# Seven products for a fourth pair of K tiles in every up strip, and two weight remainders made by an adding transfer

## The reference

```python
h += 0.5 * post(SwiGLU_1(pre(h)))      # swiglu(x) = (silu(g) * u) @ w_down, [g, u] = x @ w_up
h +=       post(Mixer(pre(h)))
h += 0.5 * post(SwiGLU_2(pre(h)))
```

## Time and profile before

| | us |
|---|---|
| median of 3 runs | 2366.02 (2365.82 to 2367.51) |
| the profiled execution | 2365.93 |
| its span, first to last instruction | 2364.2 |
| PE, DVE, ACT, POOL busy | 2349.9, 1823.2, 1265.4, 207.0 |
| share of the 16 DMA engines: SP's queue, GpSimd's queue | 59.5%, 3.5% |

### The profile page before, as it was taken

How to read it: one execution, slowest core, us unless ns; L and a number is a source line. 1 busy time by engine, 2 the same in 40 slices (tenths; PEclk the granted TensorE clock), 3 DMA queues, 4 the chain that set the end, 5 groups by cost and what they waited for, 6 DMA issues and landing times. The chain is left out here.

```text
span 2364.2 us, 34093 instructions
## 1 busy us (share of the span) xinstructions
PE 2349.9 (99%) x10579; PEld 1938.5 (82%) x10579; DVE 1823.2 (77%) x2163; ACT 1265.4 (54%) x1519; POOL 207.0 (9%) x402
## 2 busy tenths in 40 slices
PE   9999999999999999999999999999999999999998
PEld 7888888888888888888888888888888888888887
DVE  5999999978876655656675767665799999997886
ACT  6555555555545554454555544544655555555553
POOL 1212112110000000000000000000021212111000
PEclk9999999999999999999999999999999999999999
DMA  7666676665676565565565566666666666666665
GB/s 236 218 212 206 216 222 215 220 214 192 207 242 210 159 182 172 160 188 158 178 200 192 195 195 203 194 240 198 204 210 225 213 214 207 218 213 214 205 204 196
DMA packets 267183, 481.64 MB, mean 204 GB/s; under 512 B 21217, under 2 KB 54673, under 8 KB 265457
## 3 DMA queue, kind: packets, MB, share of 16 engines
q1 hardware_dynamic: 252752, 453.04, 59.5%
q0 software_dynamic: 14192, 27.73, 3.5%
q10 hardware_dynamic: 176, 0.07, 0.0%
HBM read 462.93 MB, written 6.29 MB: 198 GB/s over the span
## 5 line engine op out<-in xcount | busy, mean ns | idle before, releaser
L1382 ACT ACTIVATE w_hi<-w_raw 128x1024 fp32r<-128x1024 f32 (+1 forms) x848 | 857.4, 1015 | 926.1 <-PE acc L843 627.9
L1778 DVE TENSOR_TENSOR w_lo<-w_raw,w_hi 128x1024 fp32r<-128x1024 f32 (+1 forms) x848 | 984.2, 1164 | 420.0 <-ACT w_hi L1382 415.5
L841 PE MATMUL acc<-w_hi,xT_hi 128*128 128x512 f32 x1376 | 540.9, 393 | 1.2 <-DVE w_lo L1778 1.0
L843 PE MATMUL acc<-w_hi,xT_lo 128*128 128x512 f32 x1376 | 535.9, 389 | 0.0
L842 PE MATMUL acc<-w_lo,xT_hi 128*128 128x512 f32 x1376 | 535.7, 389 | 0.0
L841 PEld LDWEIGHTS acc<-w_hi,xT_hi 128*128 128x128 f32 x1376 | 258.3, 188 | 56.7 <-issue 3.0
L843 PEld LDWEIGHTS acc<-w_hi,xT_lo 128*128 128x128 f32 x1376 | 258.3, 188 | 54.4
L842 PEld LDWEIGHTS acc<-w_lo,xT_hi 128*128 128x128 f32 x1376 | 258.4, 188 | 52.2
L753 POOL DMA_DIRECT2D act_raw<-blocks x352 | 174.9, 497 | 736.3 <-DVE blocks L2114 646.9
L841 PE MATMUL acc<-w_hi,act_hi 128*128 128x512 f32 x560 | 218.2, 390 | 0.1
L842 PE MATMUL acc<-w_lo,act_hi 128*128 128x512 f32 x560 | 217.9, 389 | 0.0
(11 more groups left out here) (321 smaller groups left out, 2866.0 us busy)
## 6 DMA issues: line engine op xcount, KB each, us to landing
w_raw<-in_ffn_up_dram SPq DMA_DIRECT2D x352, 512.0 KB, 4.2
w_raw<-in_ffn_down_dram SPq DMA_DIRECT2D x176, 512.0 KB, 4.2
w_raw<-in_w_gate_dram SPq DMA_DIRECT2D x96, 512.0 KB, 4.4
w_raw<-in_w_in_dram SPq DMA_DIRECT2D x72, 512.0 KB, 3.7
w_raw<-in_w_in_dram SPq DMA_DIRECT2D x128, 256.0 KB, 3.0
w_raw<-in_w_ret_out_dram SPq DMA_DIRECT2D x32, 512.0 KB, 4.1
w_raw<-in_w_out_dram SPq DMA_DIRECT2D x32, 512.0 KB, 4.5
act_raw<-blocks POOLq DMA_DIRECT2D x352, 32.0 KB, 3.8
```

The source lines that it names most:

```text
L841: pe.matmul(pair[m][:, :], xh, wh, start=(first and kk == 0), stop=False)
L843: mm = pe.matmul(pair[m][:, :], xl, wh, start=False, stop=(last and kk == KG - 1))
L1382: act.activation(w_hi[:, s, cols], w_raw[:, s, cols], ACT.Copy).then_inc(w_rounded, 1)
L1778: dve.tensor_tensor(w_lo[:, s, cols], w_raw[:, s, cols], w_hi[:, s, cols].bitcast(f32), ALU.subtract).then_inc(w_split, 1)
```

## The change

Four K pairs of every up strip are quads: groups 5+6, 7+8, 10+11, 12+13 (slots 1+2, 3+0, 2+3, 0+1). The plain groups are gate 0 to 3 and upper 4, 9, 14, 15.

Groups 9 and 14 ("added" groups) take another way. GpSimd loads their raw weights into buffers of their own (`far_raw`) once PE has used the same group of the strip before. ACT rounds from there into `w_hi`, and earlier (at n = 1 and n = 7) writes the negated rounded part into `far_lo` in one more activation. Then a transfer on GpSimd's queue adds `far_raw` to `far_lo`, which gives raw - hi, the remainder; PE waits for it at the group. DVE skips these two groups, SP only counts them as landed. GpSimd's order in a strip is: two loads, the 16 transfers of the hidden strip, two adding transfers.

Left out of the diff below: buffer addresses and semaphores; the token sums of four pairs instead of three (two transposes more in the section `first` of each SwiGLU); the slices of `w_raw` that `sum13` and `sum24` read, now that one quad lies in slots 3 and 0; the wait of `hidden_hi` in the last strip, on quad 2 instead of 1.

```diff
@@ -51,9 +51,12 @@
-QUADS = ((5, 6, 5), (9, 10, 6), (12, 13, 7))
-PLAIN_GATE = ((0, 0), (1, 1), (2, 2), (3, 3), (4, 4))
-PLAIN_UP = ((7, 0), (8, 1), (11, 2), (14, 3), (15, 4))
+QUADS = ((5, 6, 4), (7, 8, 5), (10, 11, 6), (12, 13, 7))
+ADDED = {9: 1, 14: 7}
+ADDED_NEGATE = {at: n for n, at in ADDED.items()}
+ADDED_AT = {n: j for j, n in enumerate(ADDED)}
+PLAIN_GATE = ((0, 0), (1, 1), (2, 2), (3, 3))
+PLAIN_UP = ((4, 0), (9, 1), (14, 2), (15, 3))
 NQUAD = len(QUADS)
...
@@ -532,13 +544,15 @@
         DQ_B = [{nu: j for j, (ng, nu, k) in enumerate(quads)} for quads in DOWN_QUADS]
-        T_SLOT = (1, 0, 1)
+        T_SLOT = (0, 1, 0, 1)
...
@@ -645,8 +678,14 @@
                             sp.sem_inc(slot_summed, 1)
-                        k, half = source[n]
-                        load(f"up{f}", i, n, up[f][k][:, :, ds(i * STRIP + STRIP + half, STRIP)])
+                        def cols(n):
+                            k, half = source[n]
+                            return up[f][k][:, :, ds(i * STRIP + STRIP + half, STRIP)]
+                        if n in ADDED:
+                            sp.wait_ge(w_split, group(f"up{f}", i, n) + 1)
+                            sp.sem_inc(w_landed[n % SLOTS], 16)
+                        else:
+                            load(f"up{f}", i, n, cols(n))
                     sp.wait_ge(t_summed, 3 * (quad(f, i, NQUAD - 1) + 1))
...
@@ -753,6 +792,21 @@
+            def load_far(f, i, n):
+
+                j, k = ADDED_AT[n], dict(PLAIN_UP)[n]
+                pool.wait_ge(w_used, group(f"up{f}", i, n) - 2 * GD + 1 + SLOTS)
+                pool.sem_inc(far_begun, 1)
+                pool.dma_start(far_raw[j][:, :].rearrange("p (kk n) -> p kk n", kk=KG),
+                               up[f][k][:, :, ds(i * STRIP + STRIP + FFN, STRIP)]).then_inc(far_landed[j], 16)
+
+            def add_raw(f, i, n):
+
+                j = ADDED_AT[n]
+                pool.wait_ge(far_negated[j], strip_no(f"up{f}", i) + 1)
+                pool.sem_inc(far_begun, 1)
+                pool.dma_start(far_lo[j][:, :].bitcast(f32), far_raw[j][:, :], accum_op=ALU.add).then_inc(far_added[j], 16)
+
             scaled = {"n": 0}
...
@@ -785,8 +839,13 @@
             rsqrt("pre0", rs_pre[:, 0, :])
-            with pool.Fori(0, NUP) as p:
-                turn_hidden(0, p)
+            with pool.Fori(0, NST) as i:
+                for n in ADDED:
+                    load_far(0, i, n)
+                turn_hidden(0, i)
+                for n in ADDED:
+                    add_raw(0, i, n)
+            turn_hidden(0, NST)
             wait_strip_read(pool, "up0", NST - 1, 1)
...
@@ -970,11 +1034,9 @@
                 three(gate[0][:, :], *x(1), *w(ng, 1), False, last).then_inc(w_used, 1)
-                if first:
-                    pe.wait_ge(acc_read[pair_of(sec, 1)], strip_in_pair(sec, i, 1) + 1)
                 pe.wait_ge(w_split, group(sec, i, nu) + 1 + SLOTS)
                 pe.wait_ge(s_split, f + 1)
-                three(upper[0][:, :], *s(3), *w(nu, 1), first, False).then_inc(w_used, 1)
+                three(upper[0][:, :], *s(3), *w(nu, 1), False, False).then_inc(w_used, 1)
                 pe.wait_ge(t_split, 2 * quad(f, i, j) + 1)
...
@@ -1113,13 +1175,18 @@
                             s, k = n % SLOTS, KG * up_of[n]
+                            if k == 0:
+                                pe.wait_ge(acc_read[pair_of(sec, 1)], strip_in_pair(sec, i, 1) + 1)
                             pe.wait_ge(w_split, group(sec, i, n) + 1 + SLOTS)
+                            if added(sec, n):
+                                pe.wait_ge(w_rounded, group(sec, i, n) + 1)
+                                pe.wait_ge(far_added[ADDED_AT[n]], 16 * (strip_no(sec, i) + 1))
                             for kk in range(KG):
                                     mm = three(acc[pair_of(sec, 1)][m][:, :], xT_hi[:, k + kk, rows], xT_lo[:, k + kk, rows],
-                                               w_hi[:, s, cols], w_lo[:, s, cols], m == 1 and k + kk == 0,
+                                               *weights_of(sec, n, cols), k + kk == 0,
                                                n == 2 * GD - 1 and kk == KG - 1)
...
@@ -1374,6 +1441,12 @@
                     s = n % SLOTS
+                    if added(sec, ahead):
+                        j = ADDED_AT[ahead]
+                        act.wait_ge(far_landed[j], 16 * (strip_no(sec, i) + 1))
+                        act.wait_ge(w_used, group(sec, i, ahead) + 1)
+                        act.activation(w_hi[:, s, :], far_raw[j][:, :], ACT.Copy).then_inc(w_rounded, 1)
+                        return
                     act.wait_ge(w_landed[s], group_landed(sec, i, ahead))
...
@@ -1568,12 +1641,19 @@
                         round_group(sec, i, n)
+                        if n in ADDED_NEGATE:
+                            j = ADDED_AT[ADDED_NEGATE[n]]
+                            act.wait_ge(far_landed[j], 16 * (strip_no(sec, i) + 1))
+                            act.wait_ge(w_used, group(sec, i, ADDED_NEGATE[n]) - 2 * GD + 1 + SLOTS)
+                            act.activation(far_lo[j][:, :], far_raw[j][:, :], ACT.Copy, scale=-1.0).then_inc(far_negated[j], 1)
                         if n in T_AT:
...
@@ -1774,8 +1854,12 @@
                 s, cols = n % SLOTS, w_cols(sec, i, n + SLOTS)
+                if added(sec, n + SLOTS):
+                    return
+                groups = 2 if added(sec, n + SLOTS + 1) else 1
                 dve.wait_ge(w_rounded, group(sec, i, n + SLOTS) + 1)
-                dve.tensor_tensor(w_lo[:, s, cols], w_raw[:, s, cols], w_hi[:, s, cols].bitcast(f32), ALU.subtract).then_inc(w_split, 1)
+                dve.tensor_tensor(w_lo[:, s, cols], w_raw[:, s, cols], w_hi[:, s, cols].bitcast(f32),
+                                  ALU.subtract).then_inc(w_split, groups)
```

More of the change, by code:

```diff
@@ L254, in hybrid_trunk @@
         s_lo = sb("s_lo", [P, 4, NQUAD, P], f32r, at=s_x)
-        s_hi = sb("s_hi", [P, 4, NQUAD, P], f32r, at=s_x + 16 * NQUAD * P)
-        assert s_x + 32 * NQUAD * P <= r_end
+        s_hi = sb("s_hi", [P, 4, NQUAD, P], f32r, at=x_at - 4 * MT * D)
+        assert s_x + 16 * NQUAD * P <= r_end
+        far_raw = [sb("far_raw0", [P, KG * STRIP], f32, at=s_x + 16 * NQUAD * P),
+                   sb("far_raw1", [P, KG * STRIP], f32, at=r_hi - 4 * KG * STRIP)]
+        far_at = x_at - 4 * MT * D + 16 * NQUAD * P
+        far_lo = [sb(f"far_lo{j}", [P, KG * STRIP], f32r, at=far_at + 4 * KG * STRIP * j) for j in range(len(ADDED))]
+        assert s_x + 16 * NQUAD * P + 4 * KG * STRIP <= r_end and far_at + 8 * KG * STRIP <= x_at
         h_scaled = sb("h_scaled", [P, S_TILES * P], f32, at=r_hi)
@@ L396, in hybrid_trunk @@
         hid_split = sem("hid_split")
+        far_landed = [sem(f"far_landed{j}") for j in range(len(ADDED))]
+        far_negated = [sem(f"far_negated{j}") for j in range(len(ADDED))]
+        far_added = [sem(f"far_added{j}") for j in range(len(ADDED))]
+        far_begun = sem("far_begun")
         h_parked = sem("h_parked")
@@ L547, in w_cols, with t_row, added, strip_no @@
             return slice(STRIP, KG * STRIP) if half else slice(0, KG * STRIP)
+        def t_row(j, y):
+            swapped = QUADS[j][0] % SLOTS == SLOTS - 1 and y < 2
+            return 1 - y if swapped else y
         def t_pair(a, j, pair):
             return a[:, T_SLOT[j], 2 * pair:2 * pair + 2, :]
+        def added(sec, n):
+            return sec in ("up0", "up1") and n in ADDED
+        def strip_no(sec, i):
+            return NST * ("up0", "up1").index(sec) + i
         T_AT = {ng - 3 + pair: (j, pair) for j, (ng, nu, k) in enumerate(QUADS) for pair in range(2)}
@@ L563, in gate_group, with weights_of @@
             return (MERGE_GATE0 if n in MERGE_GATE0 else MERGE_GATE1)[n]
+        def weights_of(sec, n, cols):
+            if added(sec, n):
+                return w_hi[:, n % SLOTS, cols], far_lo[ADDED_AT[n]][:, cols]
+            return w_hi[:, n % SLOTS, cols], w_lo[:, n % SLOTS, cols]
         def weights(sec, n):
@@ L815, in _ @@
             rsqrt("pre2", rs_pre[:, 2, :])
-            with pool.Fori(0, NUP) as p:
-                turn_hidden(1, p)
+            with pool.Fori(0, NST) as i:
+                for n in ADDED:
+                    load_far(1, i, n)
+                turn_hidden(1, i)
+                for n in ADDED:
+                    add_raw(1, i, n)
+            turn_hidden(1, NST)
             wait_strip_read(pool, "up1", NST - 1, 1)
@@ L938, in scaled_transposes @@
                 pe.wait_ge(h_scaled_ready, f + 1)
-                for b, tiles in ((2, range(0, 2)), (3, range(2, S_TILES))):
+                for b, tiles in ((2, range(0, 4)), (3, range(4, S_TILES))):
                     claim(f"s{f}", b)
@@ L962, in tt @@
                 def tt(y):
-                    return t_hi[:, T_SLOT[j], y, :], t_lo[:, T_SLOT[j], y, :]
```

(3 more changed lines are left out.)

24 lines of the change are left out of this document (14 added, 10 removed).

## The result

The changed kernel takes **2477.52 us** in the median (2473.13 to 2482.43, 4 runs), against 2366.77 (2365.82 to 2367.79, 4 runs) for the kernel before: ratio 1.047, 95% interval 1.0457 to 1.0482. It is 111 us slower, where 36 were forecast, and lies above the range. The span of the profiled execution grew by 114.8, from 2364.2 to 2479.0.

The account below looks back on a forecast made before the run. PE was taken as the bound, DVE next in the up strips. Per strip 40.80 + 0.82 + 0.74 + 0.90 = 43.26 against 41.48; over 20 strips 35.6, plus 0.5, gives 2402 us, range 2379 to 2445.

Parts of the forecast that it names:

- Direction: Whole kernel: slower with chance 0.85, same 0.07, faster 0.08.
- the first stall: PE's sixth product of quad 0 waits 0.82 us a strip, as DVE makes quad 1's sums ahead of `t_lo`.
- The second stall: PE in quad 2, waiting for `t_lo` pair 1: 0.74 us from DVE's order plus 0.90 for a load, each strip.
- The order's part: Quad 2: `sum13` and `sum24` of quad 3 stand ahead of `t_lo` pair 1 on DVE, 0.74 us a strip.
- the load of group 11: DVE's `sum13` of quad 2 waits for this load: 0.9 us a strip, bounds 0 and 3.2.
- the token sums: Four more token-sum transposes on PE in the two `first` sections: 0.5 us for all, two matmul pitches.
- The adding transfer's length: GpSimd's transfer for group 9 takes 6 us and has 7.4 before PE wants it, so no wait.
- the first rival: Group 9's adding transfer is late and PE waits there: 2437 or 2499 us; chance 0.10 beyond 2448, 0.05 inside.
- The rule of the Trainium skill: GpSimd's DMAs wait while VectorE holds the shared port pair; prediction said the trace doesn't bear it out here.
- Being ahead elsewhere doesn't help: DVE's work in a strip's first half is counted from PE's own start, so being ahead elsewhere gains nothing.

Follow-up runs that it names:

- Experiment 7: Changed kernel with group 9's adding transfer sent ahead of the 16 hidden-strip transfers and each up strip's last two DVE multiplications left out: 2389.21 us.
- Experiment 1: Changed kernel with only GpSimd's order changed: group 9's adding transfer goes ahead of the 16 transfers of the hidden strip: 2408.73 us.
- experiment 2: Changed kernel with the adding transfers left out and their counter raised instead, so remainders of groups 9 and 14 aren't computed: 2407.58 us.
- experiment 3: Changed kernel with the four quads alone: no GpSimd loads or adding transfers, groups 9 and 14 as every other group: 2414.26 us.
- experiment 4: Changed kernel put back to three quads, with added remainders for groups 8 and 14, their transfers behind the 16: 2439.33 us.
- experiment 9: Early adding transfer, last two multiplications left out, and only 8 of 1024 columns made of up strips' remainders 3, 4 and 7, from the changed kernel: 2370.7 us.

## Why the prediction was wrong

**Direction and the first stall: right.** Slower, with 0.85. PE's sixth product of quad 0 stalls by 0.79 to 0.87 us in 15 of the 18 periods (0.94 to 1.23 in the others), predicted 0.82, for the reason given: the counted queue of DVE from its start in the strip. Experiment 7 removed just this stall by 1.44 us less of DVE.

**The second stall's place: right; its size: half.** It is at quad 2. The order's part, 0.74, is what experiments 1 and 2 show (0.65 to 0.9 where the load isn't late).

**The step that failed first is the load of group 11**: I took 0.9 with bounds of 0 and 3.2, and said that the adding transfer beside it would be the reason for the upper one. It was: the wait is 2.6 to 2.8, of which 2.5 reach PE, so the stall is 0.74 + 2.5 = 3.24, as the rows have it. The transfer leaves at 16.4 on the clock, the load at 17.0, and the load takes 6.2 us. Experiment 1 moves only the transfer; the load takes 3.8, and the wait becomes 0.21. I had the value at the upper end from rows (512 KB ahead at the DMA engines' rate, 1.7 us; measured 2.4) and chose by the wrong row: today's 0.87 was of a load with another load, but no adding transfer, beside it. With 2.5 the sum would have been 44.86 a strip, 68 us, 2434.

**The term that was missing is the clock.** A stall was counted at its length. In 17 of the 18 periods there was a stall of 3.2 us or more, and in 13 of them the clock fell, at some time between 1.3 us before PE's restart and 1.4 behind it: 1.4 us a strip on average over the 18, some 26 us in all. Behind the stalls of 0.7 to 1.7 of experiments 1, 2, 3 and 7 (in the 18 periods) slow matmuls made 0.1 to 0.6 us a strip, little more than the restarts; at those of 2.0 to 2.9 of experiment 4 the clock fell in some. So the error in the load came back once more as clock: 2434 and 20 x 1.4 is 2462. The 15 us that are left are the next points, the waits at group 9 and small gaps.

**The first sections and first strips: 0.5 us were taken for the token sums, and 1.8 each for the two first strips; measured 17.8 outside the periods.** In the profile after, the first strip of each SwiGLU has stalls of 3.25 and 1.8 (the clock fell at one of them), and 3.3 are GpSimd's DRAIN at the end. What I left out: DVE's work on the token sums grew with the number of quads, and it stands in DVE's queue ahead of the hidden strip. `s_lo`, its last part, before and after:

```profile
60.27 1.75 DVE L2136 TENSOR_TENSOR s_lo<-s_raw,s_hi 128x1536 fp32r<-128x1536 f32 x1
```

```profile
63.63 2.29 DVE L2225 TENSOR_TENSOR s_lo<-s_raw,s_hi 128x2048 fp32r<-128x2048 f32 x1
65.83 1.40 DVE L2231 SCALAR_TENSOR_TENSOR hid_sb<-acc,rs_pre,gate_sb 128x512 f32<-128x512 f32 x2
```

Counted from the first strip's start (57.37 before, one period ahead of 98.85; 59.5 after), `s_lo` ends some 1.7 us later; 0.54 of it is its own growth, the rest lies ahead of it. The first strip was already 0.7 behind the repeated ones at that place before. So DVE begins the first strip late, and PE stalls there by 3.2 to 3.4 us at quad 0, which is 0.86 and these 2.4, in every version with four quads in this order but the lightest, experiment 9 (2.4 and 2.3). I had argued from PE's matmul pitches and not from DVE's queue, against my own rule for the strips. The DRAIN had no term at all.

**The adding transfer's length: right.** 6 us predicted, 6.2 measured (4.7 to 9.3), and no wait in 17 of 20 strips. In three PE did wait for it, twice over 4 us; that is the first rival's mechanism as an outlier, 10.1 us in sum. The rule of the Trainium skill ("SBUF — State Buffer", section "SBUF: two separate sides") on the port pair that DVE and GpSimd share did not show itself: GpSimd's transfers of the hidden strip took 0.50 us to issue and the adding ones 0.86 to 0.94, beside a DVE almost without a gap. The prediction left out a condition: the section ties the rule to DVE instructions in a 2-port mode, and no run here shows whether these two-input instructions are such. From the Trainium skill ("DMA: Bandwidth & Descriptors", section "Anatomy of one DMA") the estimates were 3.2 and 4.4; the medians measured, 4.8 to 7.2 by run and group, are over both.

**"Being ahead elsewhere doesn't help"** holds, but being behind does hurt (experiment 2): once the load of group 17 comes too late for the shorter strip, DVE's clock is no longer reset by its wait at the boundary. That adds 0.35 to 0.7 us to quad 0's stall in 8 of the 18 periods of experiment 2 and in 5 of experiment 1, and is one reason why 1 and 2 are no faster although their second stall is small.

Not settled: why the load of group 17 comes no earlier in the shorter strips of experiments 1 and 2; why the clock fell at a stall of 3.2 us in some strips and not in others; why PE waits for `act_lo` behind the last strip of a SwiGLU (up to 2.6 us in the list of waits); and some 4 us outside the 18 periods, of which 1.9 lie ahead of the first SwiGLU's first section.

## What to carry to other kernels

An engine that is second at 94% has no room for a product that moves work to it: the fourth quad saves PE 0.68 us a strip and asks DVE for 4.2, of which the added remainders take 2.3 off again, and the one other order that was tried was slower still. Before a transfer is put on a free queue, look at what leaves within the same microsecond, and whether the next wait of the tight engine is for that. And count a stall at more than its length if it reaches some 3 us, for PE may come back at half speed.

## What the runs showed of the hardware

An adding transfer of 512 KB within SBUF took GpSimd 0.86 to 0.94 us to issue and landed after 4.8 to 7.2 us (medians by run and group). A load of the same size issued 0.6 us behind it took 6.2 us; with the adding transfer sent 8 us earlier, 3.8.

PE's stalls in the up strips, over all eleven profiles: none of 0.6 to 1.8 us was accompanied by a fall of the granted clock, of 21 between 2.0 and 2.9 us 8 were, and of 51 of 3.0 us or more 39, whether a DMA or an idle addition on DVE had caused them. In the profile after, a fall cost 1.2 to 1.8 us in slow matmuls (0.43 us apart instead of 0.2267), and 2.5 to 3.0 in the five periods in which the clock had fallen 0.6 us or more before PE's restart.

GpSimd's closing DRAIN took 4.2 us with 384 transfers issued, 6.0 with 424 and 8.2 with 464.
